# Indirect writes of the gates with two in flight in place of six

## The reference, cut to what matters

```
eidx = ...   # (frames, 128) numbers of the chosen experts
gate = softmax(sc)                       # (frames, 128)
a    = einsum('nd,ned->ne', x, u_emb[eidx])
coef = gelu(a) * gate
out  = einsum('ne,ned->nd', coef, v_emb[eidx])
```

## Time and profile before

| | us |
|---|---|
| median of 3 runs | 1741.58 |
| lowest, highest | 1740.88, 1742.72 |
| profiled execution | 1741.91 |
| its span | 1740.1 |
| PE busy | 1703.1 |
| POOL busy | 916.6 |
| DVE busy | 1109.5 |
| ACT busy | 576.9 |

### The profile page before, as it was taken

How to read it: one execution, slowest core, us unless ns; L and a number is a source line. 1 busy time by engine, 2 the same in 40 slices (tenths; PEclk the granted TensorE clock), 3 DMA queues, 4 the chain that set the end, 5 groups by cost and what they waited for, 6 DMA issues and landing times.

```text
span 1740.1 us, 23687 instructions
## 1 busy us (share of the span) xinstructions
PE 1703.1 (98%) x7926; PEld 1405.0 (81%) x7926; DVE 1109.5 (64%) x2997; ACT 576.9 (33%) x925; POOL 916.6 (53%) x828
## 2 busy tenths in 40 slices
PE   7999999999999999999999999999999999999997
PEld 6877877878888878888888888888888888888886
DVE  4259968544789864444444444444788888888886
ACT  4333225334322322222222222224333333333333
POOL 3644400002344007777777777771777777777710
PEclk9999999999999999999999999999999999999999
DMA  5322231115677645445547444444999999999991
GB/s 161 105 61 61 61 71 48 44 61 206 210 262 245 217 136 145 146 143 147 143 146 244 147 144 146 143 147 149 384 391 385 368 370 365 374 375 367 368 334 49
DMA packets 182675, 351.05 MB, mean 202 GB/s; under 512 B 35600, under 2 KB 118928, under 8 KB 182448
## 3 DMA queue, kind: packets, MB, share of 16 engines
q1 hardware_dynamic: 147776, 282.74, 49.0%
q0 software_dynamic: 34816, 67.41, 10.8%
HBM read 289.04 MB, written 61.02 MB: 201 GB/s over the span
## 4 chain that ended last, share of the span: by engine, by line
PE 63%; DVE 0%; issue 0%; DVEq 0%; ACT 0%
PE psum L399 21%; PE psum L398 21%; PE psum L400 21%; DVE mixed L2022 0%; DVE mixed L1999 0%; DVEq L1946 0%; DVE rstd_final L812 0%; DVE rstd_final L810 0%; DVE rstd_final L816 0%; DVE rstd_final L814 0%; DVE rstd_final L808 0%; ACT rstd_final L2133 0%; DVE rstd_final L2008 0%; DVE rstd_final L2006 0%
## 5 line engine op out<-in xcount | busy, mean ns | idle before, releaser
L2208 POOL DMA_INDIRECT gate_map<-gate_total,gate_at x384 | 403.6, 1051 | 205.3 <-DVE same_expert L1953 114.7
L398 PE MATMUL psum<-x_hi,ts_hi_u 128*128 128x512 f32 x1024 | 399.7, 390 | 4.0 <-PEq L1568 2.2
L400 PE MATMUL psum<-x_hi,ts_lo_u 128*128 128x512 f32 x1024 | 399.1, 390 | 0.0
L399 PE MATMUL psum<-x_lo,ts_hi_u 128*128 128x512 f32 x1024 | 399.1, 390 | 0.0
L1456 DVE TENSOR_TENSOR ts_lo_u<-ts_raw_u,ts_hi_u 128x1024 fp32r<-128x1024 f32 x116 | 142.3, 1226 | 341.3 <-ACT ts_hi_u L1451 338.6
L398 PE MATMUL psum<-v_hi,c_hi 128*128 128x512 f32 x768 | 298.8, 389 | 0.0
L399 PE MATMUL psum<-v_lo,c_hi 128*128 128x512 f32 x768 | 298.8, 389 | 0.0
L400 PE MATMUL psum<-v_hi,c_lo 128*128 128x512 f32 x768 | 298.8, 389 | 0.0
L1487 ACT ACTIVATE ut_out_u<-psum 128x512 f32<-128x512 f32 x128 | 76.5, 598 | 495.7 <-PE psum L400 495.7
L2113 ACT ACTIVATE v_hi<-v_raw 128x1024 fp32r<-128x1024 f32 x128 | 135.8, 1061 | 312.5 <-PE psum L400 312.5
L398 PEld LDWEIGHTS psum<-x_hi,ts_hi_u 128*128 128x128 f32 x1024 | 192.6, 188 | 44.8 <-issue 2.7
(11 more groups left out here) (242 smaller groups left out, 2321.4 us busy)
## 6 DMA issues: line engine op xcount, KB each, us to landing
ts_raw_u<-in_peer_u SPq DMA_DIRECT2D x128, 512.0 KB
v_raw<-in_peer_v SPq DMA_DIRECT2D x128, 512.0 KB, 6.0
gate_map<-zeros SPq DMA_DIRECT2D x32, 768.0 KB, 6.5
up_acts<-ut_out_u SPq DMA_DIRECT2D x128, 192.0 KB, 1.9
act_in<-up_acts SPq DMA_DIRECT2D x128, 192.0 KB, 6.3
gate_in<-gate_map SPq DMA_DIRECT2D x128, 192.0 KB, 6.7
raw_in<-in_w_in SPq DMA_DIRECT2D x56, 256.0 KB, 2.8
ts_raw_wq<-in_peer_wq SPq DMA_DIRECT2D x16, 512.0 KB, 6.4
```

The source lines that it names most:

```text
L398: nc.tensor.matmul(out, l_hi, r_hi, start=first, stop=False)
L399: nc.tensor.matmul(out, l_hi, r_lo, start=False, stop=False)
L400: return nc.tensor.matmul(out, l_lo, r_hi, start=False, stop=last)
L2208: nc.gpsimd.indirect_dma_start(gate_cells, bass.IndirectOffsetOnAxis(places["gate_at"][:, b, j:j + 1], 0), dn.total[:, b, j:j + 1], None). ...
```

## The change

One constant. It sets the number of semaphores `scattered`, the semaphore that each write counts up, the one that it waits for, and the counts that SP waits for before the gates are read (16 x 384 / IN_FLIGHT on each).

```
@@ -1900,7 +1900,7 @@
     FIRST_ROW = 10
     PER_TILE = 4
     assert PER_TILE * TILES >= DENSE_BLOCKS * SLOTS
-    IN_FLIGHT = 6
+    IN_FLIGHT = 2
     OUTS = 2 * DENSE_BLOCKS
     EARLY = RING
     ndense = NB - DENSE_BLOCKS
```

## The result

The changed kernel takes 1862.99 us in the median of four runs (1862.42 to 1867.06), the kernel before, beside it, 1741.55 us (1740.88 to 1742.72). The ratio is 1.0702, 95% interval 1.0683 to 1.0720: slower by 121 us. Forecast were 1875 us, range 1825 to 1960. One caution on the experiments further down: each group of them ran beside the kernel before, and in three of the four groups that kernel itself took 1837 to 1861 us in place of 1742, so a time there is compared only inside its own group.

What follows compares the result with a forecast made beforehand. PE, busy 98%, was taken to bound the kernel. Last write's landing 1335 plus 4.9 us to PE plus 1.5 for the clock, less 1208.3, gave 133 us more, so 1875 us; range 1825 to 1960 us.

Steps and rivals of the forecast that it cites:

- Writes in a period: Gate writes on POOL beside the up products: 2.8 per 5.44 us period, bounds 2 to 3.
- The cycle of the prediction: Up phase: per 5.44 us, two writes held by a 3.3 us DMA burst; three writes fit if the next passes, else two.
- Rival (a): Up phase: bursts average out, 3.33 writes in a period, 1804 us; chance 0.12 for 3.0 to 3.8.
- (b): Up phase: the write ahead of the store is held nearly always, two in a period, 1982 us; chance 0.18 for 2.0 to 2.5.
- When the writes end: POOL: 275 writes out by 1187 us, 109 left at 1.36 us each, 148 us more.
- E: Landing of the last gate write, forecast at 1335 us.
- The wake-up of 0.27 us: POOL: time from the end of what it waits for to its next start, 0.27 us.
- The slack: Behind the last gate write: some 20 us before SP feels a delay, about 8 us more before PE does.
- rival (d): Gate writes: the wait is hidden, the last write may land up to about 1203 us, 1741.6 us; chance 0.06.
- From the last write to PE, 4.9 us: Before the down phase: SP's wake-up 0.2, first gate load 2.4, DVE and ACT 2.15, to PE 0.1 us.
- The clock, 1.5 us: PE at the start of the down phase: resuming after idleness at a lower granted clock costs 1.5 us.
- What the profile was to show: Changed kernel: POOL idle some 150 us on write DMA, about 206 writes, threes, SP waiting, one PE gap, unchanged down phase.

Runs made afterwards that it cites:

- e1: One write in flight instead of six, against the kernel before: 2293.78 us.
- e10: Three writes in flight instead of six, against the kernel before, third time: 1746.28 us, ratio 1.0030.
- e9: Kernel before, six in flight, with a POOL memset of 128 x 384 and a wait for it ahead of each write: 1885.45 us, ratio 1.0823.
- e3: Kernel before with its six semaphores, but each write waits for the one two places back: 1863.81 us, ratio 1.0144.
- groups 1, 2 and 4: Sets of follow-up runs, each on one chip beside the kernel before, which took 1836.70, 1840.61 and 1860.71 us.
- group 3: Set of two follow-up runs beside the kernel before, which took 1742.03 us; same chip as group 4.
- e5: The kernel before, unchanged, run for its profile: 1835.41 us.
- e2: Three writes in flight instead of six, against the kernel before, first time: 1814.27 us, ratio 0.9865.
- e4: Two in flight, loads of up tiles beside the writes cut to the first eighth, against the kernel before: 1818.97 us.
- e6: Three writes in flight instead of six, against the kernel before, second time: 1818.67 us, ratio 0.9868.
- e12: Kernel before with two in flight for the first 48 writes, then six, second time: 1863.48 us, ratio 1.0027.
- e8: Kernel before with two in flight for the first 48 writes, then six, first time: 1849.57 us, ratio 1.0059.
- e7: Kernel before with two in flight for the first 96 writes, then six, first time: 1856.42 us, ratio 1.0115.
- e11: Kernel before with two in flight for the first 96 writes, then six, second time: 1865.74 us, ratio 1.0055.

## Why the prediction was right, point by point

**Writes in a period.** 2.8 were forecast, with 2 and 3 as bounds; 212 writes in 400 us are 2.88, and from the first write to 1187 us it is 2.93. By periods of the 98 loads: 49 with three writes, 26 with two, 21 with four, 2 with one. The cycle of the prediction had no place for four; had these 21 been threes, the mean would be 2.7. So the cycle is right for half of the periods, and that the mean comes so near to 2.8, a choice that no row gave, is in part luck. Rival (a) wanted 245 writes, (b) 147. The place where I had to choose, whether the write just ahead of the store gets through, went mostly the way I took it, though not quite as I put it: a write at the store's own time, 0.4 us before it to 0.2 us behind it, is down 2.6 to 3.2 us after its issue, not 2.1. One that starts 0.4 to 2.6 us behind the store is held to the end of the burst: whatever its own start, nearly all of these are down 4.5 to 5.5 us behind the store, 4.9 in the median. Those of 0.4 to 1.2 us behind it thus took 3.5 to 5.5 us.

The Trainium skill's 2.0 us plus bytes for a DMA from GpSimd (DMA: Bandwidth & Descriptors, section Anatomy of one DMA — SWDGE (gpsimd) path) agrees with e1's writes with nothing beside them, 2.1 us, but not with the median of 2.8 us beside the bursts, nor with the 6.8 us of the longest.

**When the writes end.** 288 were out by 1187.0 us, not 275, and 96 were left, not 109. Their pace was 1.378 us, 1.36 forecast. E is 1319.28 + 2.1 = 1321.4 us instead of 1335. Thirteen writes fewer at 1.36 us are 17.7 us, their pace gives back 96 x 0.018 = 1.7, and another 2.1 is the landing of the last write, which the sum had left out: it took the end of the issues for E. Together 14 us earlier, more than the whole miss of 12 us; the two errors of this term have opposite signs.

**The wake-up of 0.27 us.** Start of a write less landing of the one two before is 0.266 us where POOL waits for nothing else.

**The slack.** The prediction's 20 us to SP and 8 more to PE are counted from the last issue. From the last landing, 1174.32 + 2.1 = 1176.4 us, it is 17 us to SP at 1193.8 and 27 us to the 1203 us of rival (d), and e10 bears out the latter. The sum does not use it.

**From the last write to PE, 4.9 us.** Mis-sized: 1327.72 - 1321.4 = 6.3 us. The term that failed is the first gate load, 2.4 us by the earlier trace rows. The first gate loads of the kernel after:

```profile
DMA to landing us min/median/max: 3.9/4.1/5.8
```

They were issued from 1321.49 us on. In the kernel before POOL's first gather came 15 us after them, at 1208.70; here POOL had nothing left to wait for and issued a gather at 1320.55 and another at 1321.83, right beside the load. I had read the price of a load from a place without this neighbour. e10 bears that out: there the gathers begin 3.7 us behind the first gate load, it takes 2.4 us, and the whole way is 4.9 us. In e9, as in the kernel after, a gather goes out 1 us ahead of it, and the way is 1348.48 - 1342.0 = 6.5 us. DVE and ACT then took 1327.12 + 0.55 - 1325.51 = 2.16 us, 2.15 forecast.

**The clock, 1.5 us.** PE in the kernel after, first 3 us of the down phase (columns as in the earlier trace rows):

```profile
1327.70:1330.70 3.00, 2.98 (x7) 2.40 (x8) 3.00 (x5) 2.41 (x5) 0.00 (x0) 0.50 1.00 341
```

After 119 us of idleness the granted clock is 0.50, 1.2 GHz, for seven matmuls, the later ones 0.43 us apart in place of 0.227; by 1331.1 they are at full pace. Seven times 0.2 us is 1.4, and the down phase took 533.4 us from its first matmul against 531.8 before: 1.6. The price read after an idle 2.2 us held after 119. It is not the same each time: in e9, after 140.9 us, eleven matmuls come at this level, and its down phase takes 534.3 us, 2.5 more than before.

**The sum.** 1875 forecast; 13.6 less for E and 1.4 more for the return give 1862.8 against 1863.0 measured. PE's later start, 119.5 us, and the clock, 1.6, make the whole difference of the spans, 121.0 us.

**What the profile was to show.** Threes on the period, SP's wait (127.7 us), one hole on PE and the same down phase are there. 150 us of idle time released by the write DMA are not: the profile puts only 92.6 us there, and the rest of the 144.6 us of added idle time under DVE, PE and issue, since a wait for several semaphores is put down to one of them.

**Not foreseen.** That the 121 us depend on the surroundings. Two in flight took the same 1863 us in the first measurement and in e3, but the kernel before was 1742 us in the one and 1837 in the other, so the same depth costs 7.0% there and 1.4% here. The trace that the prediction was read from shows no sign of it.

## What to carry to other kernels

How far the depth of posted writes may be cut was set here by the slowest landing in a period, not by the mean or the best: lay the writes over the bursts of the other queue and count how many places are blocked at once. Then ask when the last one is needed; with an undisturbed up phase three in flight ended at the edge of that slack and cost 0.3%, two ended 118 us past it and cost 7%. Price what follows a delayed event with the neighbours that it will have then: an engine that waited for nothing else runs its next work right behind it.

## What the runs showed of the hardware

**Small indirect writes beside bursts.** 512 bytes in 32 packets take 2.1 us alone (158 writes of e1, all within 0.04 us). Beside a store of 256 KB and a load of 512 KB every 5.44 us their median is 2.8 us in the kernel after. Those issued 0.4 to 1.2 us behind the store take 3.5 to 5.5 us, since a write that falls into the burst is down only at its end.

**A disturbance beside fast indirect writes.** In groups 1, 2 and 4, but not in group 3 nor at the first measurement, gelus start up to 7 us behind the matmul that they wait for in e5 (median 0.8 in 700 to 1100 us), and up to 9 to 20 us in e2, e4 and e6. Up tiles take 6 to 15 us, and single ones 18 us (e6), 23 and 25 (e12, e8), 48 and 51 (e7, e11); the last four begin 14 to 18 us behind the switch from two to six, with gelus 26 to 55 us behind. Beside up products it was seen only while writes are issued at a mean of 30 or more in 50 us: in the kernel before, with three in flight, with two in flight and small loads (e4, 260 writes in 400 us), and after the switch in e7, e8, e11 and e12. It was not seen at 28 or fewer in 50 us: in e3, in e1, and ahead of the switch in those four. It shows 7 to 18 us after the switch and ends with the last write, but for 5 us in the down phase of e12. That e4 has it with two in flight speaks for the rate and against the depth. The longest delays fall where the DMA engines are nearly idle and POOL issues writes without a pause (e7, 849 to 892 us), so it is not the bytes in the DMA queues. What it is that is shared, and why two groups on one chip differ in it (1742 against 1861 us for the same kernel), stays open. So no depth is best in all groups: three in flight is 1.3% faster than the kernel before in groups 1 and 2 and 0.3% slower in group 3.
